# Low halves of two weight units moved from VectorE to GpSimd around a norm, their high halves made earlier, and one tile's transposes moved into the middle of a unit

## What is computed

```python
def rmsnorm(x, w):
    y = x * lax.rsqrt(jnp.mean(x * x, axis=-1, keepdims=True) + RMS_EPS)
    return y * w

# end of the first layer
f = (gelu(f_gate) * f_val) @ w_ffn_down
x = x + rmsnorm(f, ffn_post_norm)
# beginning of the second layer
h = rmsnorm(x, norm_pre)
cols = h @ w_in
mem_kv = rmsnorm(mem, norm_mem) @ w_mem_kv      # does not depend on x
mk, mv = split(mem_kv, 2)
```

## Time and profile before

| | |
|---|---|
| median of 3 runs | 857.1 us (856.79 to 857.69) |
| the profiled execution, its own time | 858.77 us |
| the profiled execution, span of its instructions | 856.9 us |
| granted TensorE clock, mean | 0.997 of full speed |
| TensorE matmuls busy | 839.4 us (98% of the span) |
| VectorE busy | 625.2 us (73%) |
| ScalarE busy | 510.1 us (60%) |
| GpSimd busy | 74.8 us (9%) |
| DMA, mean | 173 GB/s |

### The profile page before, as it was taken

The page is one execution under the profiler, slowest core; times in us unless marked ns, Lnnn a source line. Parts: engine busy times, 40 slices in busy tenths (PEclk is TensorE's granted clock), DMA queues, the critical chain, the costliest instruction groups (busy, mean ns, idle before and its releaser), DMA issues. The chain is left out here.

```text
span 856.9 us, 14493 instructions
## 1 busy us (share of the span) xinstructions
PE 839.4 (98%) x5726; PEld 772.4 (90%) x5726; DVE 625.2 (73%) x1130; ACT 510.1 (60%) x839; POOL 74.8 (9%) x76
## 2 busy tenths in 40 slices
PE   8999999999999999999999899999999999999996
PEld 6999999999989999999999699999899888888885
DVE  5887987998877866666665868778745566776765
ACT  6665778665377756555666878754544443645453
POOL 0100002001020211111111200140000020000000
PEclk9999999999999999999999999999999999999999
DMA  8658443457455665655555365654433243355641
GB/s 290 234 171 292 151 148 121 147 202 293 145 178 187 223 202 175 196 178 193 172 196 172 129 216 170 238 159 150 147 103 118 78 140 103 120 201 195 197 148 49
DMA packets 40587, 148.45 MB, mean 173 GB/s; under 512 B 4652, under 2 KB 5320, under 8 KB 39880
## 3 DMA queue, kind: packets, MB, share of 16 engines
q1 hardware_dynamic: 40520, 147.54, 51.1%
HBM read 146.44 MB, written 1.08 MB: 172 GB/s over the span
## 5 line engine op out<-in xcount | busy, mean ns | idle before, releaser
L1872 DVE TENSOR_TENSOR t_wl<-t_raw,t_wh 128x1024 fp32r<-128x1024 f32 x258 | 313.7, 1225 | 102.4 <-ACT t_wh L1303 101.2
L1303 ACT ACTIVATE t_wh<-t_raw 128x1024 fp32r<-128x1024 f32 x258 | 270.9, 1059 | 107.7 <-PE bank L631 57.7
L629 PE MATMUL bank<-t_hh,t_wh 128*128 128x256 f32 x1136 | 327.9, 289 | 1.3 <-DVE t_wl L1872 1.2
L631 PE MATMUL bank<-t_hh,t_wl 128*128 128x256 f32 x1136 | 321.3, 283 | 0.0
L630 PE MATMUL bank<-t_hl,t_wh 128*128 128x256 f32 x1136 | 321.3, 283 | 0.0
L629 PEld LDWEIGHTS bank<-t_hh,t_wh 128*128 128x128 f32 x1136 | 217.6, 192 | 4.3 <-DVE t_wl L1872 2.0
L630 PEld LDWEIGHTS bank<-t_hl,t_wh 128*128 128x128 f32 x1136 | 217.7, 192 | 0.9
L631 PEld LDWEIGHTS bank<-t_hh,t_wl 128*128 128x128 f32 x1136 | 217.6, 192 | 0.0
L634 PE MATMUL bank<-t_wh,t_br 128*128 128x512 f32 x384 | 123.2, 392 | 0.0
L1887 DVE SCALAR_TENSOR_TENSOR t_arena<-bank,t_par,t_arena 128x255 f32<-128x255 f32 (+2 forms) x184 | 75.3, 475 | 45.4 <-ACT t_arena L1308 45.0
L634 PE MATMUL bank<-t_wh,t_hh 128*128 128x512 f32 x224 | 91.5, 408 | 3.2 <-DVE t_wl L1872 3.2
(11 more groups left out here) (151 smaller groups left out, 845.7 us busy)
## 6 DMA issues: line engine op xcount, KB each, us to landing
t_raw<-in_ws SPq DMA_DIRECT2D x258, 512.0 KB, 3.9
t_br<-decay SPq DMA_DIRECT2D x1, 2048.0 KB, 8.8
t_arena<-in_post SPq DMA_DIRECT2D x3, 512.0 KB, 5.1
t_arena<-gates SPq DMA_DIRECT2D x1, 1536.0 KB, 10.5
t_x<-in_xin SPq DMA_DIRECT2D x2, 512.0 KB, 4.8
t_bd<-in_bd SPq DMA_DIRECT2D x1, 1024.0 KB, 8.6
t_x<-in_xtok SPq DMA_DIRECT2D x1, 1024.0 KB, 6.5
t_arena<-in_mem SPq DMA_DIRECT2D x1, 1024.0 KB, 8.6
```

Source lines behind the costliest of these rows:

```text
L629: e.matmul(o, wh, xh, start=first, stop=False, skip_group_check=True)
L631: return e.matmul(o, wl, xh, start=False, stop=last, skip_group_check=True)
L1303: e.activation(WH[q % NS][:, :], RAW[q % NR][:, :], ACT.Copy, bias=0.0, scale=1.0).then_inc(*hi.now(q))
L1872: e.tensor_tensor(WL[q % NS][:, :], RAW[q % NR][:, :], WH[q % NS][:, :].bitcast(F), SUB).then_inc(*lo.now(q))
```

## The change

For the two units of `mk3` the low half is made by GpSimd, at the end of `mem_low(2, ...)` in its list, with a counter of its own, `g_lo`. VectorE skips them. Whoever waited for these two units' low halves (TensorE, and SyncE for the fetches five units later) waits for `g_lo`. In ScalarE's list the high half of mk3a stands one norm step earlier, behind the squares of the post norm's tile 1, first column half. The high half of mk3b takes the place in which mk3a's stood. The transposes of tile 0 move from the front of mk3b to its middle, between the matmuls for token tile 0 and those for token tile 1.

```diff
@@ tallies
-        hi, lo, unit = tally("split_hi"), tally("split_lo"), tally("unit")
+        hi, lo, g_lo, unit = tally("split_hi"), tally("split_lo"), tally("split_lo2"), tally("unit")
@@ helpers
+        def split_low(q):
+            return (g_lo if FIRST["mk3"] <= q <= LAST["mk3"] else lo).of(q)
@@ sp_program
-                e.wait_ge(*lo.of(q - NR))
+                e.wait_ge(*split_low(q - NR))
                 fetch(q)
@@ pe_program
             def split_ready(q):
-                e.wait_ge(*lo.of(q))
+                e.wait_ge(*split_low(q))
...
                     e.wait_ge(*g_mh.of(2, 2 * i + j))
-                    if i == 1 and j == 1:
-                        turn_tile(0)
                     for tt in range(2):
                         m = turned(f"mk{2 + i}", u, 4 * i + 2 * j, Hh, Hl, i == 0 and j == 0, i == 1 and j == 1, (tt,))
                         if i == 1 and j == 1 and tt == 0:
                             m.then_inc(*p_tok.now("mk3"))
+                            turn_tile(0)
                     m.then_inc(*unit.now(u))
@@ act_program, second_norm
                 walk.ahead(q + 1)
                 post_squares(post, 1, 0)
+                walk.ahead(q + 2)
                 x_squares(post, pre, 0, 0)
                 post_squares(post, 1, 1)
                 root(post, 0, 1)
                 x_squares(post, pre, 0, 1)
                 root(pre, 1, 0)
-                walk.ahead(q + 2)
+                walk.ahead(q + 3)
                 x_squares(post, pre, 1, 0)
                 x_squares(post, pre, 1, 1)
-                walk.ahead(q + 3)
                 scaled(pre, 0)
                 root(pre, 1, 1)
                 walk.ahead(q + 4)
@@ dve_program
             def split(q):
+                if FIRST["mk3"] <= q <= LAST["mk3"]:
+                    return
                 e.wait_ge(*hi.of(q))
@@ pool_program
             mem_low(2, LAST["fd11"])
+            for q in range(FIRST["mk3"], LAST["mk3"] + 1):
+                e.wait_ge(*hi.of(q))
+                tt(WL[q % NS][:, :], RAW[q % NR][:, :], WH[q % NS][:, :].bitcast(F), SUB).then_inc(*g_lo.now(q))
             walk.cols("mk2", True)
```

## The result

The changed kernel takes **861.4 us** (median of 4 executions, 860.87 to 861.86) against 857.1 us: 1.0042 times as long, 95% interval 1.0029 to 1.0055. The forecast was 859.3 us, in a range up to 860.3. The direction was right, and the forecast loss of 2.2 us was half of the measured one.

A forecast was written before the change was run, and what follows sets the result against it. Bound: TensorE's waits on VectorE's low halves, then the turned tile's passage through ScalarE and VectorE. Chain 2.42 us late, less 0.33 slack, plus 0.11 restart, gave 2.2: 857.1 + 2.2 = 859.3 us; range 856.2 to 860.3, forecast's own 858.8 to 860.3.

The forecast's parts named there:

- two waits of TensorE on VectorE: TensorE idles 1.59 us before mk2b and 1.65 us before mk3a, each released by VectorE's low half of that unit.
- the chain of the turned tile: Tile 0's transposes, ScalarE's high parts, VectorE's low parts and splits up to vu1a; 0.33 us slack, 2.42 us late.
- the waiting GpSimd goes in at the change of instructions: GpSimd's subtraction enters ahead of VectorE's next instruction, making mk2b's low half 2.18 us late; chance 0.58.
- mk2b starts at 480.91, mk3a 2.85 later at 483.76: TensorE's restart after the late low half of mk2b, with no wait before mk3a.
- blocking: GpSimd and VectorE subtractions exclude each other, at mk2b's split and tile 1's additions; 2.2 us late at 500.
- VectorE keeps its turn: Rival: at 477.46 VectorE's split goes first and GpSimd waits; gain about 0.4 us, 856.7 us; chance 0.18.
- One block only: Rival: first block as forecast, second GpSimd subtraction comes after the additions; loss 1.6 us, 858.7 us; chance 0.10.
- Part 5: Tile 0's transposes in the middle of mk3b hide 1.4 us of the wait and cost 0.27 us.

The follow-up runs named there:

- The holds: Changed kernel with GpSimd's first subtraction held until VectorE made mk2b's low half, its second until the last residual addition: 857.37 us, ratio 1.0001.
- the second block alone: Changed kernel with only GpSimd's first 1024-wide subtraction held until mk2b's low half is made: 857.74 us, ratio 1.0006.
- the one profile with 2.10 us: Changed kernel with GpSimd making each low half in four pieces of 256 columns: median 858.64 us, ratio 1.0010; this profiled execution 858.67 us.

## Why the prediction was wrong

**What held.** The bound (two waits of TensorE on VectorE, and the chain of the turned tile close behind) is confirmed by the kernel with only the transposes moved: forecast 1.1, measured 1.3. That GpSimd and a two-tensor VectorE instruction exclude each other, and that the waiting GpSimd goes in at the change of instructions, gave 3.4 us for mk2b's split and 3.0 and 2.7 us for GpSimd's; the trace has 3.36, 2.88 and 2.68. GpSimd's 2.41 us was exact. The holds show that this is the cause of the whole loss, the clock's part included: with them it goes to 0.2 us, and TensorE's idle time back to 1.59.

**Which step failed.** The prediction says: "mk2b starts at 480.91, mk3a 2.85 later at 483.76". It priced mk2b's twelve matmuls at the clock of before, right behind an idle time that it had itself forecast at 3.8 us. The granted clock was 0.51 there, and mk2b took 5.29 us. The whole sum stood on what VectorE and ScalarE did, and TensorE had become the late engine: the transposes were ready to run at 487.96 (ScalarE's `scaled`, 486.37 + 1.59, forecast 488.11) and ran at 490.45. What came through to the end was 497.42 - 495.57 = 1.9 us over the kernel with extra matmuls in the wait, and 0.11 a restart is in both. So 4.1 us is 2.2 of blocking (forecast 2.2) and 1.9 of clock (forecast 0).

**What the profile before had of it.** It has the lower clock in its first stretches, behind five microseconds in which TensorE was busy for 3.48. It does not say behind which idle time the clock falls, but the forecast idle time of 3.8 us was over twice the 1.65 us behind which it was seen to stay:

```profile
5.00:10.00 5.00, 3.48 (x18) 1.00 (x16) 3.45 (x9) 4.45 (x10) 0.00 (x0) 1.00 1.00 330
10.00:15.00 5.00, 3.88 (x20) 3.88 (x20) 4.70 (x7) 3.78 (x6) 0.00 (x0) 0.66 1.04 414
```

The Trainium skill has this in TensorE: Matmul & The Clock Gate, "Part 1: The HAM clock gate": a TensorE that idles is throttled to 1.2 GHz. This trace agrees (0.51 behind 3.73 us), and the prediction did not weigh it.

**The rivals.** "VectorE keeps its turn" is refuted by the 3.36 us. The order that it stood for, brought about by holds, gave 857.3 and not the 856.7 that was worked out for it, because mk3b still waits 0.56 us for GpSimd. "One block only" was worked out at 1.6 without the clock, for the first block, and the changed kernel has both (3.36 and 3.53 us). The reverse case, the second block alone, costs 0.4 us.

**Part 5.** For the kernel as changed the transposes in the middle of mk3b were forecast to cost 0.27 us. With the clock down, their place at the front is 0.9 us better at vu1a (496.41 less 495.48), where two traces have TensorE at mk3b at the same time.

## What to carry to other kernels

Before work goes from VectorE to GpSimd, list which VectorE instructions fall beside it. Those with two SBUF tensors can be held up by a whole GpSimd instruction, also when their turn comes back to back, and so was `scaled` with one. Hold the GpSimd instruction until the urgent one is done, and put it beside VectorE work that reads PSUM. The holds alone took a loss of 4.4 us to 0.2; leaving mk3b's low half on VectorE and giving GpSimd vu0b's instead, held, made it a gain of 1.6. And when a forecast makes TensorE's idle time longer, price what follows it at the lower clock as well.

## What the runs showed of the hardware

- TensorE's granted clock stayed at 1.00 behind idle times of 1.59 and 1.65 us in this stretch. It fell to 0.5 in the one profile with 2.10 us (by the mean clock not in all executions of that kernel) and in all three with 3.73 to 3.76 us. In the profile after it fell during the idle time; in the other three only when work had resumed, 0.2, 1.2 and 1.5 us later, and in the two profiles of the changed kernel it cost 0.8 us (496.41 less 495.57) and 1.9 (497.42 less 495.57). With 14 throw-away matmuls of 3.33 us in the same place it did not fall.
- A 128 x 1024 float32 subtraction takes GpSimd 2.41 us alone and 2.7 to 2.9 when it must first wait for VectorE; it holds back a VectorE instruction with two SBUF tensors by 2.15 us (3.36 less 1.21), and six with one PSUM operand and one SBUF tensor not at all (1.64 us with it and 1.65 without).
- VectorE's multiplication of one 128 x 512 SBUF tensor by a 128 x 1 factor is held back as well: 2.02 us instead of 0.49, ending 0.28 us after GpSimd's subtraction. Its 128 x 512 `tensor_tensor` with one operand in PSUM takes 0.68 us in the middle of GpSimd's first subtraction, as it does in the kernel before.
